# Sixteen gate panels of a two-block hybrid network in pairs, seven half products for eight, ahead of the attention and kept in DRAM

## What is computed

```python
def hybrid_layer(x, norm_g, w_in, ..., w_branch, w_out, layer):
    h = rms_norm(x, norm_g)
    (aq, ak, av, az, cx, cb, cc, cz, rq, rk, rv, rz, gates) = jnp.split(h @ w_in, ...)
    a = diff_attention(aq, ak, av, ...) * silu(az)
    c = short_conv(cx, cb, cc, conv_w) * silu(cz)
    r = retention(rq, rk, rv) * silu(rz)
    g = sigmoid(gates).reshape(b, s, 3, 1024)
    merged = sum(g[:, :, i] * (branch_i @ w_branch[i]))     # i = 0, 1, 2: a, c, r
    return x + merged @ w_out
```

## Time and profile before

| | |
|---|---|
| median of three executions | 3644.6 us |
| lowest, highest | 3640.57, 3646.79 us |
| the profiled execution's own time | 3645.22 us |
| its span, first to last instruction | 3643.4 us |
| busy, share of the span | PE 98%, DVE 50%, POOL 38%, ACT 30% |
| mean granted clock of TensorE | 0.993 |
| HBM traffic over the span | 57 GB/s |

### The profile page before, as it was taken

The page is one execution under the profiler, slowest core; times in us unless marked ns, Lnnn a source line. Parts: engine busy times, 40 slices in busy tenths (PEclk is TensorE's granted clock), DMA queues, the critical chain, the costliest instruction groups (busy, mean ns, idle before and its releaser), DMA issues.

```text
span 3643.4 us, 42218 instructions
## 1 busy us (share of the span) xinstructions
PE 3572.8 (98%) x16312; PEld 2779.0 (76%) x16312; DVE 1828.8 (50%) x2321; ACT 1075.5 (30%) x1811; POOL 1391.7 (38%) x670
## 2 busy tenths in 40 slices
PE   8999999999999999999999999999999999999999
PEld 6767888888878667788888887777766678786667
DVE  5774032233156675113233236884766579556653
ACT  3443111102212335100102213124555331445542
POOL 2222344432356222344343247443422255342324
PEclk9999999999999999999999999999999999999999
DMA  4110111111134111111111114311100231111022
GB/s 163 29 34 28 58 49 47 49 49 35 38 107 139 35 30 29 49 55 47 46 52 36 41 47 140 106 45 35 53 30 27 78 129 47 36 51 35 30 70 93
DMA packets 69643, 209.21 MB, mean 57 GB/s; under 512 B 7536, under 2 KB 8560, under 8 KB 68976
## 3 DMA queue, kind: packets, MB, share of 16 engines
q1 hardware_dynamic: 48960, 159.08, 14.6%
q10 hardware_dynamic: 20528, 47.91, 3.7%
HBM read 185.99 MB, written 20.97 MB: 57 GB/s over the span
## 4 chain that ended last, share of the span: by engine, by line
PE 89%; DVE 7%; ACT 2%; issue 1%; DMA 0%; POOL 0%; SPq 0%; ACTq 0%; DVEq 0%; POOLq 0%
PE psA L500 47%; PE psT L481 16%; PE psA L481 8%; PE psA L1861 3%; PE psT L1932 2%; PE psT L779 1%; PE psT L1843 1%; PE psA L734 1%; PE psT L718 1%; DVE b_wk L1315 1%; PE psT L1909 1%; PE psT L1838 1%; DVE b_wk L2388 1%; PE psT L500 1%; PE psT L1906 1%
## 5 line engine op out<-in xcount | busy, mean ns | idle before, releaser
L447 POOL TENSOR_TENSOR Whi<-stage,credit 128x1024 fp32r<-128x1024 f32 (+1 forms) x332 | 595.3, 1793 | 2204.7 <-PE psA L500 1107.9
L450 POOL TENSOR_TENSOR Wlo<-stage,Whi 128x1024 fp32r<-128x1024 f32 (+1 forms) x332 | 796.1, 2398 | 26.0
L500 PE MATMUL psA<-Hhi,Whi 128*128 128x512 f32 x2208 | 689.6, 394 | 0.4 <-DVE b_ypad L2378 0.4
L500 PE MATMUL psA<-Hlo,Whi 128*128 128x512 f32 x2208 | 680.3, 389 | 0.0
L500 PE MATMUL psA<-Hhi,Wlo 128*128 128x512 f32 x2208 | 679.8, 389 | 0.0
L500 PEld LDWEIGHTS psA<-Hhi,Whi 128*128 128x128 f32 x2208 | 413.4, 188 | 95.5 <-issue 12.1
L500 PEld LDWEIGHTS psA<-Hhi,Wlo 128*128 128x128 f32 x2208 | 414.5, 188 | 86.6
L500 PEld LDWEIGHTS psA<-Hlo,Whi 128*128 128x128 f32 x2208 | 414.5, 188 | 86.5
L481 PE MATMUL psT<-Hhi,Whi 128*128 128x512 f32 x1024 | 424.0, 414 | 8.4 <-DVE b_wk L1303 3.2
L481 PE MATMUL psT<-Hhi,Wlo 128*128 128x512 f32 x1024 | 403.5, 394 | 0.0
L481 PE MATMUL psT<-Hlo,Whi 128*128 128x512 f32 x1024 | 402.5, 393 | 0.0
(11 more groups left out here) (324 smaller groups left out, 4836.6 us busy)
## 6 DMA issues: line engine op xcount, KB each, us to landing
stage<-in_w SPq DMA_DIRECT2D x264, 512.0 KB, 3.5
stage<-in_w SPq DMA_DIRECT2D x68, 256.0 KB, 2.6
xs<-X ACTq DMA_DIRECT2D x8, 2048.0 KB, 8.5
b_wk<-xs ACTq DMA_DIRECT2D x32, 256.0 KB, 5.1
b_wk<-xs ACTq DMA_DIRECT2D x14, 512.0 KB, 4.8
rope<-in_ropes ACTq DMA_DIRECT2D x4, 1024.0 KB, 5.0
out<-b_wk ACTq DMA_DIRECT2D x8, 512.0 KB, 2.6
b_wk<-in_x ACTq DMA_DIRECT2D x4, 512.0 KB, 10.1
```

Source lines behind the costliest of these rows:

```text
L447: pool.tensor_tensor(Whi[:, b, 0:n], stage[:, b, 0:n], credit[:, 0:1].broadcast_to([P, n]), ALU.add).then_inc(s.w_hi, 1)
L450: pool.tensor_tensor(Wlo[:, b, 0:n], stage[:, b, 0:n], Whi[:, b, 0:n].bitcast(F32), ALU.subtract).then_inc(s.w_split, 1)
L500: mm = pe.matmul(dst[h], w[:, cols], r[k][:, h * HALF:(h + 1) * HALF], start=first and k == order[0] and r is rhi and w is whi, stop=last ...
```

## The change

Of a layer's 24 gates, 16 are computed in 8 pairs between the prelude and the attention's first scores. Three "opening" gates run just before them as ordinary panels, two run at the heads of merges 0 and 1 (`GATE_BEHIND`), and three stay at the end of retention (`CLOSING_GATES`). All but the last three go through DRAM (`gs`): ACT stores each after its sigmoid, and the merges fetch them back, four buffers in turn.

For a pair, the weights of the two panels are split by the halves of the contraction into `a11, a12` (first panel) and `a21, a22` (second), H by contraction halves and token halves into `b11 ... b22`. Instead of eight products of halves, 12 matmuls each, there are seven: `a11 b11`, `a12 b21`, `s2 t2`, `s1 t1`, `s3 t3`, `s4 b22` and `a22 (b21 - t2)`, with `s1 = a21 + a22`, `s2 = s1 - a11`, `s3 = a11 - a21`, `s4 = a12 - s2` and `t1 = b12 - b11`, `t2 = b22 - t1`, `t3 = b22 - b12`. The t are made once a layer (`t_sums`, `t_rest` on DVE, `t_high` on ACT into `THI`, which lies where X lies). The s are made for each pair by DVE (`weight_sums`). ACT makes each product's high part, POOL its low part, in four slots of half a panel. Three PSUM banks of `psT` or `psA`, by turns, collect the products, partly by going on accumulating in a bank after it has been copied out; ACT copies and DVE adds the rest.

The core of the diff:

```diff
+OPENING_GATES = [(0, 0), (0, 1), (0, 2)]
+PAIRED_GATES = [(0, j) for j in range(3, 8)] + [(1, j) for j in range(8)] + [(2, j) for j in (5, 6, 7)]
+GATE_BEHIND = [(2, 3), (2, 4)]
+CLOSING_GATES = [(2, 0), (2, 1), (2, 2)]
+PRODUCTS = ("a11", "a12", "s2", "s1", "s3", "s4", "a22")
+PRODUCT_BANK = (0, 1, 0, 2, 0, 2, 0)
...
+        def low_products(pool, L, p0):
+            for t in range(GPAIRS):
+                for n in range(7):
+                    N = 7 * t + n
+                    if n < 6:
+                        pool.wait_ge(s.g_hi.sem, L * s.g_hi.per + (6 * t + n + 1))
+                    else:
+                        pool.wait_ge(s.w_hi, L * NP + (p0 + 2 * t + 2))
+                    low = pool.tensor_tensor(slot(env.Wlo, N), product_source(n), slot(env.Whi, N).bitcast(F32),
+                                             ALU.subtract)
...
+            def product(L, t, n):
+                p, slot_n = PAN1["gate", *PAIRED_GATES[2 * t]], 7 * t + n
+                if n < 6:
+                    pe.wait_ge(*s.g_ready.upto(L, 6 * t + n + 1))
+                else:
+                    pe.wait_ge(s.w_split, L * NP + p + 4)
...
+                if n in (2, 4, 5):
+                    pe.wait_ge(*s.g_taken.upto(L, 7 * t + n // 2 + n % 2))
+                elif n == 6:
+                    pe.wait_ge(*s.g_sum.upto(L, 3 * t + 2))
...
+                        if t == 0:
+                            pe.wait_ge(*t_lo.upto(L, 2 * k + 1 + r))
...
+                for g in OPENING_GATES:
+                    panel(L, ("gate", *g), Hhi, Hlo)
+                for t in range(GPAIRS):
+                    for n in range(7):
+                        product(L, t, n)
+                pe.wait_ge(*s.g_sum.upto(L, 3 * GPAIRS))
+                pe.wait_ge(*s.g_taken.upto(L, 7 * GPAIRS))
                 scores(L, 0, 0)
...
             def merge(L, i):
-                with pe.Fori(0, KT) as j:
-                    panel(L, ("gate", i, 0), Hhi, Hlo, j=j)
-                    pe.wait_ge(*b_lo.upto(L, (8, 12)[i]))
-                    pe.wait_ge(*b_hi.upto(L, (8, 12)[i]))
-                    panel(L, ("branch", i, 0), Bhi, Blo, B1_TILES, j=j)
+                panel(L, ("gate", *GATE_BEHIND[i]), Hhi, Hlo)
+                pe.wait_ge(*b_lo.upto(L, (8, 12)[i]))
+                pe.wait_ge(*b_hi.upto(L, (8, 12)[i]))
+                for j in range(KT):
+                    panel(L, ("branch", i, j), Bhi, Blo, B1_TILES)
...
                 panel(L, ("gate", 2, 1), Hhi, Hlo)
                 head_squares(L, 3)
-                for j in range(2, KT):
-                    panel(L, ("gate", 2, j), Hhi, Hlo)
-                pe.wait_ge(*b_lo.upto(L, 16))
-                pe.wait_ge(*b_hi.upto(L, 16))
+                panel(L, ("gate", 2, 2), Hhi, Hlo)
...
                 for half in (0, 1):
                     act.wait_ge(*saved[half].upto(L, 16))
+                paired_gates(L)
+                act.preload_act_table_set("natural_log_exp_and_others")
                 exps(L, 0, 0)
+                for n in (0, 1):
+                    act.wait_ge(*q_saved[n].upto(L, q_saved[n].per))
...
+            def paired_gates(L):            # ACT
+                t_high(L, 0)
+                opening_gate(L, 0)
+                t_high(L, 1)
+                opening_gate(L, 1)
+                high_product(L, 0)
+                high_product(L, 1)
+                t_high(L, 2)
+                t_high(L, 3)
+                opening_gate(L, 2)
+                high_product(L, 2)
+                high_product(L, 3)
+                for t in range(GPAIRS):
+                    N, n = 7 * t, t % 2
+                    act.wait_ge(*q_saved[n].upto(L, (2 - n + t // 2 * 2) * 16))
+                    copy_product(L, t, 0, 0)
+                    high_product(L, N + 4)
+                    high_product(L, N + 5)
+                    copy_product(L, t, 2, 1)
+                    high_product(L, N + 6)
+                    copy_product(L, t, 3, 3)
+                    gate_quarter(L, t, 1, 0)
+                    high_product(L, N + 7)
+                    high_product(L, N + 8)
+                    gate_quarter(L, t, 2, 3)
+                    high_product(L, N + 9)
+                    gate_quarter(L, t, 3, 1)
+                    high_product(L, N + 10)
+                    gate_quarter(L, t, 4, 2)
+                    act.wait_ge(*s.g_taken.upto(L, 7 * t + 7))
+                    for m in (0, 1):
+                        act.dma_start(gate_spill(PAIRED_GATES[2 * t + m]), wk[:, 3 + 2 * n + m])\
+                            .then_inc(q_saved[n].sem, 16)
...
+            def paired_gates(L):            # DVE
+                dve.wait_ge(*h_lo.upto(L, 2 * KT))
+                t_sums(L, 0)
+                t_sums(L, 1)
+                t_rest(L, 0)
+                t_sums(L, 2)
+                t_rest(L, 1)
+                weight_sums(L, 0)
+                t_sums(L, 3)
+                t_rest(L, 2)
+                t_rest(L, 3)
+                for t in range(GPAIRS):
...
+                    added(0, 1, 1)
+                    added(3, 4, 3)
+                    added(1, 5, 2)
+                    weight_sums(L, t + 1)
```

More of the change, by code:

```diff
@@ L151, in panels_of_block1, with gate_panels, branch_panels @@
             out += [(("rv", h), KT, P), (("rz", h), KT, P)]
-    out += merge_panels(2)
+    out += gate_panels(CLOSING_GATES) + branch_panels(2)
     out += [(("out", j, half), KT, P) for half in (0, 1) for j in range(KT)]
     return out
[L157 to L163, removed]
+def gate_panels(gates):
+    return [(("gate", *g), KT, P) for g in gates]
+def branch_panels(i):
+    return [(("branch", i, j), B1_TILES, P) for j in range(KT)]
 def panels_of_block2():
@@ L184, in panels_of_block2, with runs @@
     return out
-def runs(panels):
+def runs(panels, paired=()):
     out, off = [], 0
@@ L191, in runs @@
         sizes = [panels[p + b][1] * panels[p + b][2] for b in (0, 1)]
-        if out and out[-1][2] == sizes:
+        seven = panels[p][0] in paired
+        if out and out[-1][2] == sizes and out[-1][4] == seven:
             out[-1][1] += 1
         else:
-            out.append([p, 1, sizes, off])
+            out.append([p, 1, sizes, off, seven])
         off += sum(sizes)
@@ L321 @@
 PAN2 = {p[0]: i for i, p in enumerate(P2)}
-RUNS1, COLS1 = runs(P1)
+RUNS1, COLS1 = runs(P1, [("gate", *g) for g in PAIRED_GATES])
 RUNS2, COLS2 = runs(P2)
@@ L420, in _ @@
                 with sp.Fori(0, DEPTH) as L:
-                    for p0, pairs, sizes, off in the_runs:
+                    for p0, pairs, sizes, off, _seven in the_runs:
                         with sp.Fori(0, pairs) as i:
@@ L438, in _ @@
                 with pool.Fori(0, DEPTH) as L:
-                    for p0, pairs, sizes, off in the_runs:
+                    for p0, pairs, sizes, off, seven in the_runs:
+                        if seven:
+                            env.low_products(pool, L, p0)
+                            continue
                         with pool.Fori(0, pairs) as i:
@@ new lines, in gate_behind, with fetch_gate @@
+            def gate_behind(L, i):
+                use = ("gate", *GATE_BEHIND[i])
+                take(L, use, BEHIND[i], ACT.Sigmoid)
+                act.wait_ge(*A.drained(L, use))
+                act.dma_start(gate_spill(GATE_BEHIND[i]), BEHIND[i]).then_inc(behind_saved.sem, 16)
+            def fetch_gate(L, i, j):
+                if j >= 4:
+                    act.wait_ge(*A.drained(L, ("branch", i, j - 4)))
+                act.dma_start(wk[:, GATES[i][j % 4]], gate_spill((i, j))).then_inc(gate_in[j % 4].sem, 16)
```

229 lines of the change are left out of this document (189 added, 40 removed).

## The result

Runs of the two kernels on one chip, in turns: before 3642.59 us (median of 4, 3638.93 to 3646.79), after **3612.66 us** (median of 4, 3610.08 to 3614.52). The ratio is 0.9917, with a 95% interval of 0.99 to 0.9934: the change takes 30 us (by the ends of the interval 24 to 36). The forecast was 3620 us, with 3602 to 3638 for the range. The profiled execution of the kernel after took 3613.21 us, its span 3611.3.

A forecast was written before the change was run, and what follows sets the result against it. PE bounds the kernel, in one unbroken chain of matmuls. Terms -43.5 + 2.2 + 13.4 + 3.0 + 0.6 = -24.3 us, off the median of 3644.6, give 3620 us; 8 in 10 range 3602 to 3638.

The forecast's parts named there:

- 192 matmuls at 0.2267 us, -43.5: Pairs of gates: 84 matmuls instead of 96, 16 pairs over two layers, 192 fewer at 0.2267 us: -43.5 us.
- Product boundaries, +2.2: Between consecutive products on PE: 112 products with waits, priced like two half panels that follow each other: +2.2 us.
- The steady loop at no cost: Steady pairs: other engines feed seven products in 19.04 us, with 2.6 us of cover for `a11`; costed at nothing.
- The opening, 5.2 of stall and 1.5 of clock a layer, +13.4: Before the first product 2, PE waits 5.2 us a layer, then loses 1.5 to a lower clock: +13.4 us.
- The entry into attention, +3: Last product to attention: scores 1.1 us later, then ACT waits for saved gates; 1.5 us a layer, +3 us.
- Merges, branches and the closing, +0.6: Merges and branches cost nothing; the second closing gate's sigmoid moves behind five issues, 0.3 us a layer: +0.6 us.
- Rival one: Opening: DVE's additions slip between POOL's instructions, T is ready by 38, no stall: 3607 us; chance 0.18.
- Rival two: Steady pairs: the next pair's weights load late, paid 16 times: 3639 us, or 3658 at 8.5 us landings; chance 0.19.
- three (waits for saves): Entry into attention: gate stores land later than 9 us, second exponentials wait, 4 us and 1.5 a layer: 3631; chance 0.15.

The follow-up runs named there:

- runs with extra writings: Against the kernel after, GpSimd wrote the low part of `a11` three times, then five times, instead of once: 3631.28 us and 3714.32 us.
- lambda edit: Against the kernel after, DVE's two operations on columns of `lam`, and the wait ahead of them, go behind `paired_gates`: 3601.5 us, ratio 0.9887.
- run without `Hlo`: Against the kernel after, the T sums are formed from `Hhi` alone, leaving out the addition of `Hlo`: 3598.43 us, ratio 0.9884.

## Why the prediction was right, step by step

- *192 matmuls at 0.2267 us, -43.5.* Held. 7 × 2.72 = 19.04 a pair in the chain.
- *Product boundaries, +2.2.* Nothing: consecutive products run without a seam. The lower end was the right one.
- *The steady loop at no cost.* Held. The order of events was right, the cover 2.08 us instead of 2.6; the runs with extra writings show that this margin alone keeps the pairs at 19.04.
- *The opening, 5.2 of stall and 1.5 of clock a layer, +13.4.* The sum was right (14.3 in the first profile, 14.7 in the second), by two errors that offset each other in part: the stall was 4.7, the clock behind it 2.5 and 2.0. The slow stretch was priced from one of 4.2 us; these lasted 5.3 and 4.0. The last T sum was put at 38.8 after the opening's start and ended at 38.4: T began 1.1 later than forecast, and the turns with GpSimd cost some 7.7 instead of 8.7 (an estimate: 35.9 us from 73.82 to 109.75, less 28.2 for the same operations where nothing is beside them). That DVE is late with T, and that its late start can be had back, is shown by the lambda edit and by the run without `Hlo`. GpSimd's part in it is read from the timelines, 2.77 us for 0.69; no run takes GpSimd away. That ACT's order behind it is a cause was wrong: moving it brought nothing, since DVE's low T parts are late next.
- *The entry into attention, +3.* 3.2 in the first profile, 1.9 in the second (295.50 and 298.07 us of attention, against 295.6 to 295.8 in all profiles of the kernel before). The second scores started 3.65 us after the last product, 3.6 was forecast, with the table load of 1.28 us in between as its row said. That is the 1.1 us a layer of the forecast; the further 0.4 for the saves is not seen. The first half panel behind the entry took 5.7 to 7.1 us in both kernels, from one execution to the next, so what is beyond 2.2 us may be chance.
- *Merges, branches and the closing, +0.6.* About nothing: -151.86 and -55.2 in layer 0 where the matmuls alone are -152.34 and -54.4.
- *Rival one (no stall, 3607).* It didn't happen by itself. With DVE's T sums shortened the stall is gone and the time is 3598.4. Of the 8.6 us below the rival's 3607, 7.3 are those by which the forecast itself lay above the kernel after.
- *Rival two (late loads) and three (waits for saves).* Neither: with twice the stores the loads land 0.2 us later in the median. The second exponentials did wait: the saves and then four small issues of ACT held them until 272.58, but PE had its half panel until 276.86. In the second profile of the kernel after the chain goes through this wait, and attention took no longer than before (295.50 in that layer).

Sum of the measured terms: -43.5 + 14.3 + 3.2 and 0.4 that no stage accounts for = -25.6 for the first block, 1.3 from the forecast. Of the 7.3 us between the forecast and the median of the runs these are 1.3; 2.0 are the kernel before, whose median was 3644.6 then and 3642.6 in these runs; the other 4 are of the size by which single executions differ, in the second block above all. So the mechanism and its price were right to 1.3 us, and the rest of the distance says nothing for or against them.

## What to carry to other kernels

Fewer matmuls are worth their full time where the chain is one unbroken piece of them, and a scheme of sums that needs other engines costs most at its start: price the first group, not the loop. Look there for waits that have nothing to do with the new work (here two operations on one column, behind which VectorE's sums stood in line); moving them was worth 11 us more, a third of what the change itself gave. In the loop, find the one chain of load, copy and split that must be ready for the next group, write down its cover, and count DMA issues as work of the engine that makes them.

## What had not been expected of the hardware

- Gaps of PE of 2.8 to 4.7 us in the paired stage were each followed by matmuls 0.43 us apart at the lower clock (granted 0.51), 7 to 12 of them behind gaps of 4.0 to 4.7 in the stretches read; behind gaps of 0.4 and 0.9 us the steps were 0.23 from the second or third matmul on.
- An issue on ScalarE's queue took 0.33 to 0.46 us alone or in twos. Four stores of 512 KB in a row took 2.88, the third 0.80 and the fourth 1.21, but four fetches of that size 1.99.
- The unchanged second block took 1298.2 to 1304.8 us from one execution to the next, a fifth of the whole effect of this change.
